# A two-block transformer on one core: layer 0's state-space powers in quarters, norm sums earlier, coefficients reordered, and an opening with the first token tile in halves and TensorE on zeros

## The reference, cut to what matters

```python
for layer in range(2):
    xn = rms_norm(h, attn_norm_g[layer])
    u_ssm, u_g, v_g, q, k, v = split(xn @ w_in[layer])
    y_ssm = s5_mixer(u_ssm, ...)           # states: x_t = a x_(t-1) + b u_t, complex; y = Re(c x) + d u
    y_sgu = spatial_gating(u_g, v_g, ...)
    y_diff = diff_attention(q, k, v, ...)  # per head: softmax - lam * softmax, then rms_norm of the output
    h = h + concat(y_ssm, y_sgu, y_diff) @ w_out[layer]
    h = h + conv_gated_mlp(rms_norm(h, ffn_norm_g[layer]), ...)
return second_block(h, ...)
```

## Time and profile before

| | us |
|---|---|
| median of three runs (983.65 to 986.6) | 984.04 |
| the profiled execution | 983.3 |
| its span | 981.5 |
| TensorE busy (PE) | 954.1 (97%) |
| VectorE busy (DVE) | 690.5 (70%) |
| ScalarE busy (ACT) | 547.4 (56%) |
| GpSimd busy (POOL) | 263.2 (27%) |

### The profile page before, as it was taken

One profiled execution on the slowest core, in us unless ns is written; L12 is line 12 of the kernel. 1 busy time (PEld: TensorE's weight loads), 2 busy tenths in 40 slices (PEclk: granted clock), 3 DMA queues, 4 the chain that ended last, 5 costly groups with the idle time before them and its releaser, 6 DMA issues.

```text
span 981.5 us, 15775 instructions
## 1 busy us (share of the span) xinstructions
PE 954.1 (97%) x6139; PEld 838.0 (85%) x6143; DVE 690.5 (70%) x1074; ACT 547.4 (56%) x900; POOL 263.2 (27%) x196
## 2 busy tenths in 40 slices
PE   5979999999999999999999999999999999999997
PEld 4867789999978887899999988899777889888886
DVE  6998658776764689676777764558575845666785
ACT  7736556665744656766655654553444454555723
POOL 4891101677800021200555400003131300000030
PEclk9999999999999999999999999999999999999999
DMA  7722355655655552556655566565545445754462
GB/s 287 230 85 87 108 174 191 186 183 174 190 190 154 173 168 86 177 168 194 184 192 183 185 192 194 184 204 175 167 149 150 142 153 169 196 167 152 147 186 84
DMA packets 48473, 165.95 MB, mean 169 GB/s; under 512 B 6544, under 2 KB 7056, under 8 KB 48400
## 3 DMA queue, kind: packets, MB, share of 16 engines
q1 hardware_dynamic: 48400, 164.95, 53.0%
HBM read 162.83 MB, written 1.05 MB: 167 GB/s over the span
## 4 chain that ended last, share of the span: by engine, by line
PE 86%; DVE 8%; ACT 2%; POOL 1%; issue 1%; DMA 0%; DVEq 0%; POOLq 0%; SPq 0%; ACTq 0%
PE PJ L605 14%; PE PJ L607 13%; PE PJ L606 13%; PE PJ L596 10%; PE PJ L598 10%; PE PJ L597 10%; DVE wlo L1710 2%; PE PJ L557 2%; PE PJ L559 2%; PE PJ L558 2%; PE T L1045 1%; PE T L1036 1%; PE S L652 1%; DVE ropeq L1821 1%; PE T L974 1%
## 5 line engine op out<-in xcount | busy, mean ns | idle before, releaser
L1710 DVE TENSOR_TENSOR wlo<-raw,whi 128x1024 fp32r<-128x1024 f32 x294 | 366.9, 1280 | 87.1 <-ACT whi L1104 84.8
L1104 ACT ACTIVATE whi<-raw 128x1024 fp32r<-128x1024 f32 x294 | 302.5, 1062 | 73.6 <-DMA raw<-weights_in 64.7
L596 PE MATMUL PJ<-xthb,whi 128*128 128x256 f32 x864 | 243.1, 281 | 0.9 <-DVE wlo L1710 0.5
L598 PE MATMUL PJ<-xthb,wlo 128*128 128x256 f32 x864 | 242.3, 280 | 0.0
L597 PE MATMUL PJ<-xtlb,whi 128*128 128x256 f32 x864 | 241.5, 280 | 0.0
L605 PE MATMUL PJ<-whi,xthb 128*128 128x512 f32 (+1 forms) x432 | 174.3, 403 | 3.6 <-DVE wlo L1710 3.6
L607 PE MATMUL PJ<-whi,xtlb 128*128 128x512 f32 (+1 forms) x432 | 167.9, 389 | 0.0
L606 PE MATMUL PJ<-wlo,xthb 128*128 128x512 f32 (+1 forms) x432 | 167.7, 388 | 0.0
L596 PEld LDWEIGHTS PJ<-xthb,whi 128*128 128x128 f32 x864 | 163.0, 189 | 1.7 <-issue 1.5
L597 PEld LDWEIGHTS PJ<-xtlb,whi 128*128 128x128 f32 x864 | 163.0, 189 | 0.2
L598 PEld LDWEIGHTS PJ<-xthb,wlo 128*128 128x128 f32 x864 | 162.9, 189 | 0.0
(11 more groups left out here) (402 smaller groups left out, 1342.1 us busy)
## 6 DMA issues: line engine op xcount, KB each, us to landing
raw<-weights_in SPq DMA_DIRECT2D x294, 512.0 KB, 3.5
rt<-bmerge_in SPq DMA_DIRECT2D x6, 256.0 KB, 4.4
xres<-x_in SPq DMA_DIRECT2D x2, 512.0 KB, 5.5
memx<-mem_in SPq DMA_DIRECT2D x2, 512.0 KB, 4.1
y_out<-xn SPq DMA_DIRECT2D x4, 256.0 KB, 2.3
rowv<-rows_in SPq DMA_DIRECT2D x1, 576.0 KB, 10.5
ptmp<-bexp_in SPq DMA_DIRECT2D x2, 256.0 KB, 6.3
cex<-cexp_in SPq DMA_DIRECT2D x2, 256.0 KB, 8.5
```

Source lines behind the costliest of these rows:

```text
L596: pe.matmul(o, a, xh[:, k, :], start=(first and f % 2 == 0), stop=False, skip_group_check=True)
L598: m = pe.matmul(o, b, xh[:, k, :], start=False, stop=last, skip_group_check=True)
L1104: act.activation(whi[:, p % HIGHS, :], raw[:, p % LOADS, :], ACT.Copy).then_inc(hi_ready, 1)
L1710: dve.tensor_tensor(wlo[:, p % LOADS, :], raw[:, p % LOADS, :], whi[:, p % HIGHS, :].bitcast(F32), ALU.subtract).then_inc(lo_ready, 1)
```

## The change

- **Coefficients**: what doesn't depend on a, are and aim over their squared length, is computed in seven instructions ahead of the scaling of tile 0; what is left is six instructions on two rows at a time, behind k's head sums instead of between low halves 9 and 10. Rows 11 and 12 of `sp_` change places, and `fold_coefficient` reads them so.
- **Quartered powers**: in layer 0 the input and output powers are made in four parts of two state groups each (`parts=4`), each step's four parts one after the other, with a wait behind the last only. Layer 1 keeps whole ones.
- **POOL's order**: k's head power ahead of `folded`.
- **VectorE's order**: k's scaling directly behind its rotary, the phase turns behind low half 12; the lambda products behind low halves 15 and 16; in both layers the sums of tile 1 ahead of the norm of tile 0, and the low half that stood between them behind the norm of tile 1.
- **Norm sums**: the norms in `AT_ONCE` (the first and the memory's) add epsilon to the first sum as soon as it is there.
- **Opening**: token tile 0 comes in two transfers of 512 columns, each square waiting for its own; TensorE makes 16 fp32 products of zeros (from `mT`, which POOL clears) ahead of the first transposes, and 11 transposes of the identity into an unused bank behind them.

```diff
-            small(xres[:, 0, :], x[0:P, :], "x_landed0")
+            for h in range(2):
+                small(xres[:, 0, 512 * h:512 * h + 512], x[0:P, 512 * h:512 * h + 512], f"x_landed0{'ab'[h]}")
...
                 if l == 0:
+                    pe.wait_ge(sem("mhalf_ready"), 2)
+                    for i in range(16):
+                        pe.matmul(B[:, 1, 0:P], mT[:, 0, :], mT[:, 1, :], start=True, stop=True)
                     norm_transposes(0, (0,))
+                    keep_busy(B[:, 1, :], 11)
...
-            act.wait_ge(sem("x_landed0"), 16)
             for half in range(2):
+                act.wait_ge(sem(f"x_landed0{'ab'[half]}"), 16)
                 squares(0, xres, 0, half)
...
+                    else:
+                        pool.wait_ge(sem("ssq_ready"), 4 * n + 2 * t + 1)
                         link(pool.tensor_scalar(ssm1[:, n, t:t + 1], ssq[:, n, 2 * t:2 * t + 1], D * EPS, None, ALU.add))
+                        pool.wait_ge(sem("ssq_ready"), 4 * n + 2 * t + 2)
...
-            link(pool.memset(mT[:], 0.0))
+            pool.memset(mT[:], 0.0).then_inc(sem("mhalf_ready"), 1)
+            pool.wait_ge(sem("mhalf_ready"), 2)
...
-            input_powers(pool, link, 0, 0, x_tile(0), ptmp)
-            input_powers(pool, link, 0, 1, x_tile(1), ptmp)
+            input_powers(pool, link, 0, 0, x_tile(0), ptmp, parts=4)
+            input_powers(pool, link, 0, 1, x_tile(1), ptmp, parts=4)
...
+            head_powers(0, 1)
             folded(0)
-            head_powers(0, 1)
-            output_powers(pool, link, 0, 0, ptmp)
-            output_powers(pool, link, 0, 1, ptmp)
+            output_powers(pool, link, 0, 0, ptmp, parts=4)
+            output_powers(pool, link, 0, 1, ptmp, parts=4)
```

The heart of the quartered form (output powers; the input powers have the same loops over three quarters of the columns):

```diff
+            w = ST // parts
+            for step in steps:
+                for at in range(0, ST, w):
+                    ...
+                    if step == 0:
+                        link(eng.tensor_tensor(o, i0, k0, ALU.mult), False)
+                    if step == 1:
+                        link(eng.tensor_tensor(tt_, i1, k1, ALU.mult), at + w == ST)
+                    if step == 2:
+                        link(eng.tensor_tensor(o, o, tt_, op), at + w == ST)
```

On VectorE:

```diff
             dve.sem_inc(sem("par_ready"), 1)
+            are, aim = col("are"), col("aim")
+            link(dve.tensor_tensor(v[16], are, are, ALU.mult), False)
+            link(dve.tensor_tensor(v[17], aim, aim, ALU.mult))
+            link(dve.tensor_tensor(v[16], v[16], v[17], ALU.add))
+            link(dve.reciprocal(v[13], v[16]))
+            link(dve.tensor_tensor(v[16], are, v[13], ALU.mult), False)
+            link(dve.tensor_tensor(v[15], aim, v[13], ALU.mult), False)
+            link(dve.tensor_tensor(v[17], aim, v[13], ALU.mult))
             norm_scale(0, xres, 0)
...
+                from_one = apw[:, :, :, :].rearrange("p c t n -> p (c t) n")[:, 0:STEP + 3:STEP + 2, :]
+                link(dve.tensor_scalar(apw[:, 0, 0, :], apw[:, 0, 1, :], -1.0, None, ALU.add))
+                link(dve.tensor_tensor(sp_[:, 22:24, :], from_one, sp_[:, 16:18, :], ALU.mult), False)
+                link(dve.tensor_tensor(sp_[:, 13:15, :], from_one, sp_[:, 15:17, :], ALU.mult))
+                link(dve.tensor_tensor(v[9], v[22], v[23], ALU.add), False)
+                link(dve.tensor_tensor(v[10], v[14], v[13], ALU.subtract))
+                link(dve.tensor_scalar(sp_[:, 11:13, :], sp_[:, 9:11, :], -1.0, None, ALU.mult))
...
-                if l == 0:
-                    lo_upto(s0 + 10)
-                    coefficients()
                 lo_upto(s0 + 11)
...
                 head_sums(1)
+                if l == 0:
+                    coefficients()
                 rotary(1, B, "k_terms", "k_rot", s0 + (14 if l else 12))
-                if l == 0:
-                    phase_turns(dve, link, 0)
-                    lo_upto(s0 + 13)
                 ...
                 if l == 0:
+                    lo_upto(s0 + 13)
+                    phase_turns(dve, link, 0)
...
+                    lo_upto(s0 + 17)
                     lambdas()
-                    lo_upto(s0 + 17)
                     scans()
...
+                diff_sums(1)
                 diff_norm(0)
-                lo_upto(s0 + 23)
-                diff_sums(1)
                 diff_norm(1)
                 lo_upto(s0 + 24)
```

More of the change, by code:

```diff
@@ L378, in fold_coefficient @@
             eng.wait_ge(sem("cex_landed"), 16 * (l + 1))
-            cr, ci, nci, ncr = (wide(sp_[:, r, 8 * l:8 * l + 8], 32, 2) for r in (9, 10, 11, 12))
+            cr, ci, nci, ncr = (wide(sp_[:, r, 8 * l:8 * l + 8], 32, 2) for r in (9, 10, 12, 11))
             re, im = cex[:, 0, :, :], cex[:, 1, :, :]
@@ L386, in fold_coefficient, with output_powers @@
                 link(eng.tensor_tensor(o, o, t, ALU.add))
-        def output_powers(eng, link, l, c, tmp, steps=(0, 1, 2)):
-            ar, ai = (wide(apw[:, c, 1:STEP + 1, 8 * l:8 * l + 8].rearrange("p t s -> p s t"), 32, 3) for c in range(2))
-            cr, nci = (wide(gpw[:, c, :, 0, :], STEP, 2) for c in range(2))
+        def output_powers(eng, link, l, c, tmp, steps=(0, 1, 2), parts=1):
             t = tmp.rearrange("p (s t h) -> p s t h", s=ST, t=STEP)
[L393 to L400, removed]
@@ L402, in input_powers @@
-        def input_powers(eng, link, l, c, x, tmp, steps=(0, 1)):
-            ar, ai = (wide(apw[:, k, 1:STEP, 8 * l:8 * l + 8].rearrange("p t s -> p s t"), 32, 3) for k in range(2))
-            br, bi = (wide(bex[:, k, :, :], STEP - 1, 2) for k in range(2))
+            w = ST // parts
+            for step in steps:
+                for at in range(0, ST, w):
+                    ar, ai = (wide(apw[:, k, 1:STEP + 1, 8 * l + at:8 * l + at + w].rearrange("p t s -> p s t"), 32, 3) for k in range(2))
+                    cr, nci = (wide(gpw[:, k, at:at + w, 0, :], STEP, 2) for k in range(2))
+                    i0, k0, i1, k1, op = ((cr, ar, nci, ai, ALU.add), (nci, ar, cr, ai, ALU.subtract))[c]
+                    o, tt_ = gpw[:, c, at:at + w, 1:STEP + 1, :], t[:, at:at + w, :, :]
+                    if step == 0:
[4 more added lines that the diff above has]
+                        link(eng.tensor_tensor(o, o, tt_, op), at + w == ST)
@@ L406, in input_powers @@
+        def input_powers(eng, link, l, c, x, tmp, steps=(0, 1), parts=1):
             xv = x.rearrange("p (s t h) -> p s t h", s=ST, t=STEP)
             t = tmp[:, 0:ST * 96].rearrange("p (s t h) -> p s t h", s=ST, t=STEP - 1)
-            o = xv[:, :, 1:STEP, :]
-            i1, k1, op = (bi, ai, ALU.subtract) if c == 0 else (br, ai, ALU.add)
+            w = ST // parts
             if 0 in steps:
                 link(eng.tensor_copy(xv[:, :, 0, :], bex[:, c, :, :]), False)
-                link(eng.tensor_tensor(o, br if c == 0 else bi, ar, ALU.mult), False)
+            for step in ([0] if 0 in steps else []) + ([1, 2] if 1 in steps else []):
+                for at in range(0, ST, w):
+                    ar, ai = (wide(apw[:, k, 1:STEP, 8 * l + at:8 * l + at + w].rearrange("p t s -> p s t"), 32, 3) for k in range(2))
+                    br, bi = (wide(bex[:, k, at:at + w, :], STEP - 1, 2) for k in range(2))
+                    i1, k1, op = (bi, ai, ALU.subtract) if c == 0 else (br, ai, ALU.add)
+                    o, tt_ = xv[:, at:at + w, 1:STEP, :], t[:, at:at + w, :, :]
+                    if step == 0:
+                        link(eng.tensor_tensor(o, br if c == 0 else bi, ar, ALU.mult), False)
+                    if step == 1:
+                        link(eng.tensor_tensor(tt_, i1, k1, ALU.mult), at + w == ST)
+                    if step == 2:
+                        link(eng.tensor_tensor(o, o, tt_, op), at + w == ST)
@@ L413, in input_powers @@
             if 1 in steps:
-                link(eng.tensor_tensor(t, i1, k1, ALU.mult))
-                link(eng.tensor_tensor(o, o, t, op))
                 eng.sem_inc(sem("xpow_ready"), 1)
@@ L1785, in coefficients @@
             def coefficients():
[L1787 to L1801, removed]
-                link(dve.tensor_scalar(v[12], v[9], -1.0, None, ALU.mult))
+                from_one = apw[:, :, :, :].rearrange("p c t n -> p (c t) n")[:, 0:STEP + 3:STEP + 2, :]
[5 more added lines that the diff above has]
+                link(dve.tensor_scalar(sp_[:, 11:13, :], sp_[:, 9:11, :], -1.0, None, ALU.mult))
                 dve.sem_inc(sem("par_ready"), 1)
```

5 lines of the change are left out of this document (2 added, 3 removed).

## The result

The changed kernel took **987.2 us**, median of nine runs (985.87 to 988.22), beside 983.62 for the kernel before on the same chip: a ratio of **1.0037 (95% interval 1.0029 to 1.0046)**. That is 2.5 us above the forecast and inside its own range, but a little slower, where "within 0.3%" had the largest chance. The profiled execution has a span of 985.4 us (981.5 before); VectorE is busy for 686.6 us (690.5), POOL for 274.6 (263.2).

What follows compares the result with a forecast made beforehand. TensorE's large waits lie early in layer 0, so the first 115 us decide; VectorE and POOL share a nearly full lock there. 983.3 + 0.9 + 1.7 - 1.7 - 0.2 = 984.0, 984.7 on the median's scale; range 976.5 to 989.5.

Steps and rivals of the forecast that it cites:

- within 0.3%: Outcome not to be told from no change, 981.1 to 987.0 us: chance 0.42, against 0.33 faster and 0.25 slower.
- The opening: Start of layer 0: split tile, early epsilon and zeros bring tile 1 to 19.8 for 21.46, 1.7 us earlier.
- The 7.9: Time in us of TensorE's first transpose behind the zero products, 8.7 before, taken at full clock.
- The input powers: Layer 0, quartered on POOL: components ready at 28.6 and 37.6; TensorE waits 2.5 us at the second input transposes.
- VectorE's and POOL's order: Layer 0 middle: K scaled at about 53 for 59.33; waits of 1.8 (K transposes), 3.2 and 0.2 (low halves 14, 15) go.
- The output powers: Layer 0, POOL's quarters ahead of the Toeplitz products: end at 79.2, 0.9 us later than before, between 77.0 and 82.4.
- the sum of 28.7: Microseconds of POOL and VectorE work the shared lock must carry from 48.3 until the output powers end, so 77.0.
- POOL starves: Rival, chance 0.18: VectorE streaks hold the lock, output powers end at 82.4 or a streak later; 989 us.
- POOL keeps up: Rival, chance 0.30: quarters run on without giving up the lock, Toeplitz at about 74, clock steady; 977.8 us.
- The clock behind it: Toeplitz products run partly at half pace after TensorE's wait of 6.7 us for POOL: 1.7 us lost.
- The end of the attention: Layer 0: second sums ahead of the first norm shorten TensorE's wait at the attention output's transposes: 1.7 us gained.
- The 0.2 of layer 1: Gain of 0.2 us in layer 1, where the squares come too late for more.

Runs made afterwards that it cites:

- one_dma: `reordered` with the first token tile in one DMA of 512 KB again, zeros and all else kept: 978.5 us, 0.9952.
- hold3: Changed kernel, quarters kept, VectorE's work behind low half 15 waiting for the third count, POOL's last output power: 985.71 us, 1.0024.
- experiment 4: Changed kernel, quarters kept, with VectorE's later work held back until POOL's output powers are done: `hold` (wait without effect) 987.52 us, `hold3` 985.71 us.
- whole_all: Changed kernel with input and output powers whole again, all else kept: 980.73 us, 0.9974.
- diff_order: Apparently the kernel before with only the new order at the end of both layers' attention (second sums ahead of first norm): 980.8 us, 0.9976.
- whole_out: Changed kernel with only the output powers whole again, input powers still in quarters: 982.24 us, 0.9990.
- hold: Changed kernel with a wait meant to hold VectorE's later work; its count was there long before, so it repeats the changed kernel: 987.52 us, 1.0048.
- quarter_alone: Kernel before with the quartered input and output powers alone; opening, orders and coefficients as before: 987.0 us, 1.0034.
- reordered: Changed kernel with whole powers and VectorE's order changed: low halves 14 and 15 between state products and sums, second maxima ahead of states: 978.99 us, 0.9955.
- opening: Kernel before with the opening alone (tile in halves, early epsilon, zero products, 11 identity transposes): 983.25 us, 1.0003.

## Why the prediction came out as it did

**The opening: right.** First transposes at 7.95 (predicted 7.9), products at 10.52 (10.7), tile 1 at 19.39 (19.8). The scaling of tile 0 began at 6.52 instead of 8.05, 1.5 earlier where 1.05 was taken; but by `one_dma` that isn't what moved tile 1. The 7.9 was met by some luck: the data was there well before 7.6 (without the zeros the transposes start at 7.16), and the zeros, which took 6.22 us, ended at 8.1. The Trainium skill (SBUF — State Buffer, summary of rules for kernel authors) asks for one transfer instead of several. The halves did land earlier here, and the rule's outcome, nothing gained from the split, holds at tile 1 (19.58 against 19.64) and at the end (0.9952 against 0.9955).

**The input powers: right, but for the clock.** Ready at 28.35 and 37.93 (predicted 28.6 and 37.6), a wait of 3.03 (2.5). I did not follow what such a wait can do: the window behind it ran at 0.50 and lost 1.5 us. The k sums ended at 46.2 for 44.7; in `hold3`, where the clock held, at 45.3, so 0.9 of this is the clock. The head power ended at 49.6 for 48.3. TensorE came to the Toeplitz products at 75.2 (82.35 less 7.17) for 72.5: 0.4 is the later start of the transposes, 1.5 the clock, 0.4 a wait for low half 15, and 0.4 stays open. I had priced such a fall at one wait and not at the other.

**VectorE's and POOL's order: right.** K scaled by 53.4 (about 53), no wait ahead of the K transposes, low half 14 in time. Only the small wait for low half 15, which was to go, is there (0.41).

**The output powers: the right mechanism, the wrong size.** This is the step that failed: "I take low half 16 and the lambdas, the ones queued first: 79.2". POOL began 1.3 us later than reckoned (head power at 49.6), so the sum of 28.7 would end at 78.3. The sum came out in total: in `hold3`, with VectorE's later items held, the head power ended at 48.7, the sum gives 77.4, and POOL ended at 77.5. In its parts that is luck: 13.7 for the output powers with their quarter overhead was 15.1, and the rest, 15.0, was 13.7. What was added to the sum was 3.8, not 2.2, and by other items than I took. Low half 16 and the lambdas added 1.0, the lambdas none of it; the scans and low half 17, which I put at nothing, added 2.8 (experiment 4). All that VectorE had queued started before POOL's last quarter ended. There was a reason to see this: each turn that POOL gives away lets VectorE get on to its next item, so as long as POOL has quarters left, nothing stops VectorE's queue short of its end. *POOL starves* came nearer in its time (82.4), but not in its mechanism: it needed streaks in which a quarter takes over 2 us, and none took more than 1.70. *POOL keeps up* failed on its condition: quarters with no wait between them took 1.64 to 1.70 one behind the other, each with a VectorE instruction let in.

**The clock behind it: right.** 1.55 us lost in the window from 82.35 (1.7 taken).

**The end of the attention: right.** 1.7 taken; alone it is worth 0.24% (2.1 us between the medians).

**The sum with measured terms:** 983.3 + 4.1 + 1.5 - 2.0 = 986.9; the profiled execution took 987.2. The 0.2 of layer 1 was not measured by itself.

**One sentence of the first part was wrong:** that a shift in the first 115 us reaches the end unchanged. In the changed kernel a later TensorE does (4.08 later at the Toeplitz products, 1.5 lost to the clock and 2.0 gained at the end of the attention make 3.6; the transposes there came 3.51 later). An earlier one doesn't. In `whole_all` the Toeplitz products started 2.7 us earlier than in `diff_order` (75.09 against 77.83), yet the attention output's transposes came at 110.86, only 0.35 earlier. VectorE was next: it ran from 58 to 92 us without a gap, and the waits for its products (1.0) and for a copy of ScalarE behind its maxima (1.1) took most of the rest. For the same reason the price of *POOL keeps up*, 977.8, was too low by 3 us: whole powers, which do what that rival asked for, gave 980.7.

## What to carry over

Where two engines take turns at a resource, the grain of an instruction decides which of them waits: keep it whole on the engine that sets the next start. (Small pieces on the other engine, which would follow from it, were not tried.) When the price of such a step is a range "up to all that the other has queued", ask what stops that queue; here nothing did, and all of it got in. Price each item by itself even so: all 5.4 us on top of POOL's measured start would have given 83.7, and the lambdas cost nothing. And before a gain on the main engine is carried to the end, look which engine has no gap in the stretch behind it.

## What the runs showed of the hardware

- Where VectorE had instructions with two inputs in SBUF one behind the other (low halves, scans), one got in between every two quarters of POOL, and these quarters took 1.6 to 1.7 us for 0.63 to 0.73. The lambda products got in too, but cost POOL nothing (0.63 a quarter). Between whole products of 1024 columns the same low halves wait longer (2.98 us against 1.76 for one, 4.54 against 2.78 for two).
- Splitting has a price of its own: four quarters take 2.40 us (2.77 in the step that adds), one whole product 1.97 (2.42).
- Waits of one length did not always cost the clock. Ahead of the second input transposes TensorE stood for 3.03 us in the changed kernel, 3.04 in `whole_out` and `hold3` and 3.02 in `hold`; from 38 to 41 us the clock was 0.50 in the first, 0.68 in the second and 1.00 in the other two. After 2.60 (`quarter_alone`) it fell, after 1.65 (`reordered`) it did not. In `opening` and `one_dma` it was 0.50 to 0.52 from 50 to 57 behind a wait of 0.7 only, where `whole_all` and `reordered`, with the same wait, had 1.00. What decides it no run here tells.
- Two transfers of 256 KB instead of one of 512 KB: the first square starts at 3.62 to 4.06 us in ten profiles and the second at 4.51 to 4.88; with the one transfer the first starts at 4.67 to 5.22 in four.
